# Moving the relative-bias products, the opening splits and one statistic in a two-layer hybrid encoder

## The reference, cut to what matters

```python
def encoder_layer(x, ...):
    h = x @ w_in                              # 1024 -> 2912 columns
    (a_q, a_k, a_v, a_g, b_cq, b_ckv, b_kr, b_g, c_q, c_k, c_v, c_g) = split(h)
    oa = window_attn(a_q, a_k, a_v, sink, t5_table) * silu(a_g)   # relative bias: t5_table[bucket(rel)]
    ob = mla(b_cq, b_ckv, b_kr, ...) * silu(b_g)
    oc = neighborhood_attn(c_q, c_k, c_v, rpb) * silu(c_g)        # relative bias: rpb
    o = concat([oa, ob, oc]) @ w_out
    return layer_norm(DEEPNORM_ALPHA * x + o, ln_g, ln_b)

def trunk(x, ...):
    x = layer_norm(x, ln_in_g, ln_in_b)
    for l in range(DEPTH):                    # DEPTH = 2
        x = encoder_layer(x, ...)
```

## Time and profile before

| | us |
|---|---|
| median of three runs | 1842.55 (1841.69 to 1842.91) |
| profiled execution, its own time | 1846.45 |
| its span, first to last instruction | 1844.7 |
| PE busy | 1798.5 (97%) |
| DVE / ACT / POOL busy | 945.6 / 772.2 / 431.5 |

### The profile page before, as it was taken

The page is one execution under the profiler, slowest core; times in us unless marked ns, Lnnn a source line. Parts: engine busy times, 40 slices in busy tenths (PEclk is TensorE's granted clock), DMA queues, the critical chain, the costliest instruction groups (busy, mean ns, idle before and its releaser), DMA issues.

```text
span 1844.7 us, 32212 instructions
## 1 busy us (share of the span) xinstructions
PE 1798.5 (97%) x12530; PEld 1467.1 (80%) x12530; DVE 945.6 (51%) x2060; ACT 772.2 (42%) x1666; POOL 431.5 (23%) x668
## 2 busy tenths in 40 slices
PE   4999999999999999999999999999999999999997
PEld 4887689889987666889989866988898766578897
DVE  6365765211425776555463476550133277565638
ACT  2345754211125666553233366441212366755510
POOL 0353402311111273001162223140111224600010
PEclk9999999999999999999999999999999999999999
DMA  6676332211124122004145552521212061200022
GB/s 232 174 248 173 107 126 92 92 46 47 47 69 124 27 65 80 1 1 149 35 155 160 155 139 70 183 92 37 67 47 69 23 149 40 95 12 2 24 81 92
DMA packets 148308, 167.16 MB, mean 91 GB/s; under 512 B 18320, under 2 KB 134416, under 8 KB 147648
## 3 DMA queue, kind: packets, MB, share of 16 engines
q1 hardware_dynamic: 145792, 157.64, 28.6%
q0 software_dynamic: 1152, 4.19, 0.6%
q10 hardware_dynamic: 1216, 3.28, 0.5%
HBM read 143.00 MB, written 32.65 MB: 95 GB/s over the span
## 4 chain that ended last, share of the span: by engine, by line
PE 91%; DVE 6%; ACT 1%; issue 1%; DMA 1%; POOL 0%; SPq 0%; DVEq 0%
PE psum L633 66%; PE psum L758 8%; PE psum L728 8%; PE psum L710 6%; DVE nmax L1147 2%; PE psum L769 1%; DVE pt_sb L1178 1%; PE psum L643 1%; DMA w_stage<-w_in 1%; PE psum L615 0%; POOL gT L1405 0%; DVE w_lo L517 0%; PE psum L596 0%; ACT w_stage L898 0%; DVE x_lo L1138 0%
## 5 line engine op out<-in xcount | busy, mean ns | idle before, releaser
L633 PE MATMUL psum<-w_hi,x_hi 128*128 128x256 f32 (+1 forms) x1344 | 380.9, 283 | 3.3 <-DVE x_lo L1138 3.3
L633 PE MATMUL psum<-w_hi,x_lo 128*128 128x256 f32 (+1 forms) x1344 | 379.2, 282 | 0.0
L633 PE MATMUL psum<-w_lo,x_hi 128*128 128x256 f32 (+1 forms) x1344 | 376.8, 280 | 0.0
L633 PE MATMUL psum<-x_hi,w_hi 128*128 128x512 f32 x816 | 325.5, 399 | 0.5 <-POOL w_lo L517 0.5
L633 PE MATMUL psum<-x_lo,w_hi 128*128 128x512 f32 x816 | 324.4, 398 | 0.0
L633 PE MATMUL psum<-x_hi,w_lo 128*128 128x512 f32 x816 | 324.4, 398 | 0.0
L517 POOL TENSOR_TENSOR w_lo<-w_stage,w_hi 128x1024 fp32r<-128x1024 f32 (+1 forms) x79 | 159.2, 2023 | 685.9 <-ACT w_hi L929 685.8
L517 DVE TENSOR_TENSOR w_lo<-w_stage,w_hi 128x1024 fp32r<-128x1024 f32 (+1 forms) x81 | 139.1, 1734 | 298.9 <-ACT w_hi L929 298.9
L633 PEld LDWEIGHTS psum<-w_hi,x_hi 128*128 128x128 f32 x1344 | 254.3, 189 | 3.9 <-DVE x_lo L1138 3.7
L633 PEld LDWEIGHTS psum<-w_lo,x_hi 128*128 128x128 f32 x1344 | 256.4, 191 | 0.2
L633 PEld LDWEIGHTS psum<-w_hi,x_lo 128*128 128x128 f32 x1344 | 253.5, 189 | 0.0
(11 more groups left out here) (148 smaller groups left out, 2602.2 us busy)
## 6 DMA issues: line engine op xcount, KB each, us to landing
w_stage<-w_in SPq DMA_DIRECT2D x48, 512.0 KB, 4.4
w_stage<-w_in SPq DMA_DIRECT2D x88, 256.0 KB, 3.4
toep<-rpb_tile SPq DMA_DIRECT2D x12, 1152.0 KB, 15.5
rpb_tile<-rpb_col SPq DMA_DIRECT2D x48, 192.0 KB
hT<-y SPq DMA_DIRECT2D x18, 512.0 KB, 5.5
y<-hT SPq DMA_DIRECT2D x18, 512.0 KB, 2.7
w_stage<-w_out SPq DMA_DIRECT2D x32, 256.0 KB, 4.1
w_stage<-w_out SPq DMA_DIRECT2D x16, 512.0 KB, 5.3
```

What stands on the lines that cost most here:

```text
L633: last = nc.tensor.matmul(out, w, x, start=(n == 0 and part != 1), stop=(n == len(pairs) - 1 and part != 0))
```

## The change

Four edits. (1) In the opening, `prompt_norm(1)` is put ahead of the two `split_low` of unit tc on DVE, half 1 of unit tc is loaded before input tile 1, and PE transposes tile t + 1 ahead of the products of tile t instead of tile t ahead of its own. (2) The T5 products stand between units ck and aq0 instead of between tc and ck, and DVE's negatives and ACT's two table writes each go one unit later. (3) The wait of PE for the negatives goes one unit later too. (4) In the last run the left statistics of a tile are taken after the sum of its o2 group instead of before that of its o3 group.

```diff
@@ PE: x_of_tile, loop over the input units
-                    if t >= 2:
-                        x_tiles(s, (t,))
+                    if 1 <= t < NTILES[s] - 1:
+                        x_tiles(s, (t + 1,))
                     for hf in range(2):
                         wait_read(pe, ("xT", s, t, hf))
...
-                    if s == 0 and i == 1:
+                    if s == 0 and i == 2:
                         pe.wait_ge(pre_const, 16 * 5)
                         wait_read(pe, ("xT", s, NT - 1, 1))
                         nc.tensor.matmul(bank[7][0:A_HEADS, :], t5_sb, onehot, start=True, stop=True).then_inc(pre_mm, 1)
-                    if s == 0 and i == 2:
+                    if s == 0 and i == 3:
                         pe.wait_ge(pre_neg, 1)
@@ DVE: opening, then the loop over the input units
                         low_part(s, t - 1)
+                        prompt_norm(t)
                         if t == 1:
                             split_low(dve, s, 0, 0)
                             split_low(dve, s, 0, 1)
-                        prompt_norm(t)
...
                     if i:
                         split_low(dve, s, i + 1, 1)
+                    if s == 0 and i == 2:
+                        dve.wait_ge(pre_mm, 1)
+                        nc.vector.scalar_tensor_tensor(out=t5_neg[:, :], in0=bank[7][0:A_HEADS, :], scalar=-1.0, in1=pen,
+                                                       op0=ALU.mult, op1=ALU.add).then_inc(pre_neg, 1)
+                        dve.wait_ge(pre_rpb, 16 * DEPTH * C_HEADS)
+                        nc.vector.tensor_scalar(pad_neg[:, :, :], pad_sb, -1.0, None, ALU.mult).then_inc(pre_neg, 1)
+                        dve.wait_ge(sink_loaded, 16 * DEPTH)
+                        link(nc.vector.tensor_scalar(nsink[:, :], sink_in[:, :], -1.0, None, ALU.mult))
...
                     if s == 0 and i == 0:
                         split_low(dve, s, 1, 1)
-                        dve.wait_ge(pre_mm, 1)
...
@@ DVE: output units
-                    if n == 3:
+                    if n == 3 and s + 1 < RUNS:
                         for m in (0, 1):
                             wait_read(dve, ("out", s, m, t))
                         left_stats(z_place(t), ln_no[s, t] - 1)
...
+                    if n == 2 and s + 1 == RUNS:
+                        for m in (0, 1):
+                            wait_read(dve, ("out", s, m, t))
+                        left_stats(z_place(t), ln_no[s, t] - 1)
@@ SP: first loads
                     load_unit(s, 0, 0)
+                    load_unit(s, 0, 1)
                     load_input(1)
-                    load_unit(s, 0, 1)
```

## The result

The change made the kernel slower: a median of 1846.35 us (1845.87 to 1847.24, 12 runs) against 1842.53 (1841.69 to 1846.09, 12 runs) of the kernel before beside it, ratio 1.0017 with a 95% interval of 1.0009 to 1.0024. That is 3.8 us, where the forecast was 0.8 less and the range ended at 1845.5. The profiled execution of the changed kernel took 1847.13 (span 1845.3), only 0.7 more than the profiled 1846.45 of before.

What follows compares the result with a forecast made beforehand. PE, busy 97% of the span, was taken as the bound. Terms -3.1 - 0.5 - 2.8 + 3.9 + 2.3 - 0.6 = -0.8 us, taken off the median 1842.55, gave 1841.7; range 1836.0 to 1845.5.

Steps and rivals of the forecast that it cites:

- Minus 2.8: Unit ck on PE: with the T5 products gone from before it, no stretch at 1.2 GHz; 2.8 us won, bounds 0 and 2.9.
- Minus 0.5: T5 products on PE: run at 2.4 GHz behind ck instead of partly at half clock; 0.5 us won, bounds 0 and 0.5.
- third rival: ck stays at 1.2 GHz, or runs outside the profile never had the fall; 2.8 not won, 1844.5 us; chance 0.14.
- Plus 3.9: PE ahead of cq: waits for cq's split weights after finishing ak; 3.9 us lost, bounds 2.6 and 5.
- E + 5.3: SP's queue: let go 2.46 us after aq0's last copy starts, then the first spread's three transfers take 2.84.
- E: Start of aq0's last copy, from which later steps are counted: 69.70 us before, about 63.3 predicted after.
- upper bound of 5: Stall ahead of cq: up to 5 us if the table writes share engines with POOL's sample-tile store and land 1 later.
- Ak split at E + 11.1: ak's weights are split 11.1 us after aq0's last copy starts, just in time for aq1's end at 11.24.
- its load is hidden under these 6.2 even at twice the 3.3: cq's load, issued when ak is split, lands within the 6.2 us until POOL's sample-tile store is issued, costing nothing.
- E + 20.8: cq's weights are split 20.8 us after aq0's last copy starts, while PE is done with ak at 16.9.
- a sign of being wrong: Stated refutations: cq starts without a wait, ak waits too, or ck is slow again.
- where I had 2.3: Clock falls in the wait for cq and slows products behind it; 2.3 us lost, bounds 0 and 2.9.

Runs made afterwards that it cites:

- cq's load clear: Changed kernel with cq's loads ahead of the second spread and the T5 table's read in SP's order: 1846.31 us, ratio 1.0014 to the kernel before.
- edits 2 and 3 alone: Kernel before with only the T5 products behind ck and the negatives, table writes and PE's wait one unit later: 1850.89 us, ratio 1.0040.
- POOL's tiles later: Changed kernel with POOL's sample tiles one unit later: 1847.58 us; with cq's loads also ahead of the second spread and T5 read: 1843.08 us.
- the changed kernel again: Changed kernel timed and profiled once more, no edit: 1846.66 us, ratio 1.0018 to the kernel before.
- edit 1 alone: Kernel before with only the opening's part of the change (tile 1 normalised sooner, transposes one tile earlier, first loads swapped): 1840.32 us, ratio 0.9987.
- the writes early: Changed kernel with ACT's table writes ahead of aq0's copies instead of behind them: 1840.05 us, ratio 0.9981 to the kernel before.
- spreads later: Changed kernel with the neighbourhood table's spreads one unit later in SP's order: 1841.31 us, ratio 0.9986 to the kernel before.

## Why the prediction was wrong

**The failed step is "Minus 2.8", the clock on ck, with the "Minus 0.5" beside it.** The rows were read rightly, but they were rows of an execution 3.9 above the median, and I made the sum against it and then took its result off the median. The two profiles of before, 1846.45 and 1842.61, differ by 3.8, and their stages show where: unit ta starts 3.86 later in the first. Of that 0.78 is already there at the end of tc (41.19 and 40.41), 0.45 is the T5 products' low clock (1.40 and 0.95), and 2.63 is ck (13.98 and 11.35). The first profile's ck:

```profile
44.28:58.26 13.98, 13.98 (x49) 0.79 0.84 269
```

The 0.78 is PE's pace too: tc's first products start 0.21 apart until 26.03 in the first profile and until 24.09 in the second, 0.12 apart after that, though the granted clock reads 1.00 over both. In the kernel as it mostly runs, there was no low clock on ck to remove: against its profile the two terms came to nothing (ck 11.41 for 11.35, the T5 products 0.94 for 0.95). I had this as half of my third rival, with 0.14; the 3.9 between the execution and the median, about the price of the stretch, was the sign that should have raised it.

**The second miss is the term "Plus 3.9", the stall: 4.95 by its measure** (0.28 ahead of ak, 4.67 ahead of cq).
- The step "E + 5.3" came as E + 5.6. SP was let go 3.69 after E, not 2.46, and the first spread took 1.94 on its queue, not 2.84. The writes behind the copy were not as quick as those at 58.46; their issue took 1.32 where it had been 0.64. This is the case that the prediction had at its upper bound of 5, writes beside POOL's store of a sample tile:

```profile
62.61 0.73 POOL L1450 DMA_DIRECT2D y<-gT  x1 [0.31 <-POOL gT L1410]
```

  With that store beside the writes SP was let go 3.66 to 3.96 after E (the changed kernel twice, cq's load clear, and edits 2 and 3 alone, where it was issued at 66.15 with E at 66.14); without it, in both kernels with POOL's tiles later, 2.48. The 2.46 of the earlier trace rows was also a short case for the kernel before, which took 3.41 in its second profile with no store near.
- "Ak split at E + 11.1" came at E + 11.4, so ak was 0.28 late. The terms as written, 9.25 + 0.6 + 1.42, add up to 11.27, already past the 11.24 of aq1.
- POOL's add started 2.92 after that (2.93 predicted) and its store was issued 6.2 after it, as predicted. The failed link is "its load is hidden under these 6.2 even at twice the 3.3": the load took 6.4 to 7.3, ACT's high part came behind it, and POOL lost 0.90. So cq was ready at E + 21.9 and not E + 20.8. With the load clear, the wait was 3.82.

**What held.** The first product came at 20.10 (20.45 predicted), tc's end at 37.58 (38.1), E at 63.17 (63.3). The T5 products took 0.94 behind ck, at granted clock 1.00. The writes' place left ak 0.28 late, which the prediction had as a sign of being wrong, and cq with a wait released by remainders, with the low clock from inside it on: 13.73 for cq against 11.24 in the profile of before without a fall, 2.5 where I had 2.3. (In the profile of the changed kernel again cq took 12.86, which is 1.6.) At the end the last sum starts right behind the last row tile, and the tail is 0.6 shorter. The timeline of DVE there, against the earlier trace rows, shows that the statistics of line 1077 no longer stand ahead of the sum (line 1372):

```profile
1836.61 1.28 DVE L1122 SCALAR_TENSOR_TENSOR gT<-gT,ln_rs,qkC 128x1024 f32<-128x1024 f32 x1
1837.81 0.41 DVE L1372 SCALAR_TENSOR_TENSOR gT<-gT,psum 128x256 f32<-128x256 f32 x1
```

**The sum again**, against the profile of before without a fall: opening -2.8, T5 products 0, ck 0, stalls +4.95, low clock behind them +2.5, tail -0.65, and +0.5 in aq0, aq1 and ak (28.6 where they took 28.1), which I had at nothing: +4.5. The spans differ by 4.5 (1845.3 and 1840.8). Of my miss of 4.6 on the median (1846.35 and 1841.7), 1.5 is the difference of profile to profile (+0.7 where I had -0.8), 1.05 of it the stall and 0.5 these three units; the other 3.1 is that the profile of before stood 3.9 above its median, and the one of after 0.8.

Two things stay open. POOL's store was not moved away from the writes by itself, since the edit that moved it moved POOL's tiles too. And whether cq's load was slowed by the spread or by the read of t5row was not told apart, since one edit moved both. The traces of layer 2 speak for the read: there SP issues none, cq's load stands 2.1 to 2.3 behind the end of a spread's issue, as here (2.16), and it landed in 3.5 to 6.2 (both profiles of the kernel before and both of the changed kernel), here in 6.3 to 7.3. Other transfers differ between the layers, so this is no proof.

## What to carry to other kernels

Before a stretch of one profiled execution goes into a sum against the median, set that execution's time beside the runs: a term as large as the distance between them may be the distance itself. Writes that a queue must wait for belong where nothing urgent is queued behind the wait; here their place was worth 6.3 us, and everything that the change meant to win. Independent work on PE pays best in an idle that is there anyway (2.1 us and steadier runs, 1840.53 to 1838.39; about 1 us is the work's own time, the rest the fall that most runs seem to have had), and an idle fed by two chains shortens little until both are moved.

## What the runs showed of the hardware

The same kernel, with the same idle of 1.70 and the T5 products behind it, lost the clock in some executions and not in others, for 3.41 or 6.83 us at 1.2 GHz; of 27 runs of before 8 had the lower mean clock. In the changed kernel ck followed the same idle without the T5 products, and neither of its two profiles has a fall there, nor has any of the six other kernels with the T5 products behind ck; of the five profiles with them behind the idle two have one (the kernel before, and edit 1 alone). So "Minus 2.8" holds, as far as these profiles go, for executions that have the fall. The waits for cq of 3.82 to 4.67 each have a fall inside them or right behind (five profiles), those of 0.45 to 2.05 have none (three). Where the T5 products do not stand behind the idle ahead of ck and cq waits 0.45 or not at all (the three kernels with them in the idle, and that with the writes early), the runs of a kernel lie within 1 us of each other, against 5 for the kernel before.

The load of cq, issued 0.65 behind the read of t5row and a spread, landed in 7.4 to 9.0 (spreads later); 2.1 behind, in the changed kernel, in 6.4 to 7.3; 4.8 and 5.4 behind, in the two profiles of the kernel before, in 5.3 to 6.1 and 3.7 to 5.4; ahead of them in 3.8 to 4.8. The load of ak, behind a spread alone, took 3.1 to 3.3. The Trainium skill (DMA: Bandwidth & Descriptors, "Specifications") asks for at least 512 B in a transfer for full rate. The spreads have runs of 128 B; ak's load shows no harm from that, and cq's is no proof of it, since the other read lay beside it.
